# Activation tiles streamed from the last token to the first, from buffers that begin 16 bytes past a multiple of 256

## The reference, cut to what matters

```python
def sq_relu_mlp(h, w_up, w_down):
    return jnp.square(jax.nn.relu(h @ w_up)) @ w_down

def conv_ffn(h, w_up, conv_w, w_down):
    up = causal_dwconv(h @ w_up, conv_w)
    a, u = up[..., :D_FF_2], up[..., D_FF_2:]
    return (jax.nn.silu(a) * u) @ w_down
```

## Time and profile before

| what | value |
|---|---|
| runs | 1120.18 and 1120.35 us, median 1120.26 us |
| span of the profiled execution | 1118.6 us, so 1.7 us less than the median of the runs |
| PE busy | 1111.2 us, 99% of the span, 9640 matmuls |
| weight loads (PEld) busy | 1093.5 us, 98%, 9640 loads |
| DVE busy | 851.5 us, 76% |
| ACT busy | 664.8 us, 59% |
| POOL busy | 252.7 us, 23% |
| DMA | 203.28 MB, mean 182 GB/s |

### The profile page before, as it was taken

One profiled execution on the slowest core, in us unless ns is written; L12 is line 12 of the kernel. 1 busy time (PEld: TensorE's weight loads), 2 busy tenths in 40 slices (PEclk: granted clock), 3 DMA queues, 4 the chain that ended last, 5 costly groups with the idle time before them and its releaser, 6 DMA issues.

```text
span 1118.6 us, 26120 instructions
## 1 busy us (share of the span) xinstructions
PE 1111.2 (99%) x9640; PEld 1093.5 (98%) x9640; DVE 851.5 (76%) x1373; ACT 664.8 (59%) x1113; POOL 252.7 (23%) x248
## 2 busy tenths in 40 slices
PE   9999999999999999999999999999999999999998
PEld 8998999999998999999999999999999999999998
DVE  7776977656687977755587699999668888999854
ACT  6566656545578665644556667666455456666544
POOL 0001400000140600011200363544211034444421
PEclk9999999999999999999999999999999999999999
DMA  9542765655653666565564455664667565665461
GB/s 323 189 151 88 220 196 189 203 197 187 166 161 98 196 199 199 161 223 188 157 188 152 150 173 170 207 201 143 199 203 228 175 213 169 202 204 178 150 211 62
DMA packets 206799, 203.28 MB, mean 182 GB/s; under 512 B 9824, under 2 KB 204768, under 8 KB 206736
## 3 DMA queue, kind: packets, MB, share of 16 engines
q1 hardware_dynamic: 206592, 202.22, 56.9%
q10 hardware_dynamic: 144, 0.20, 0.1%
HBM read 201.35 MB, written 1.05 MB: 181 GB/s over the span
## 4 chain that ended last, share of the span: by engine, by line
PE 98%; DMA 1%; DVE 0%; SPq 0%; issue 0%; ACT 0%
PE gemm L772 29%; PE gemm L774 29%; PE gemm L773 29%; PE gemm L804 2%; PE gemm L806 1%; PE gemm L805 1%; PE gemm L781 1%; PE gemm L783 1%; PE gemm L782 1%; PE score L1017 1%; PE gemm L1029 1%; DMA w_raw<-in_w_first 1%; PE score L1152 0%; PE misc L834 0%; PE gemm L1168 0%; PE score L1240 0%
## 5 line engine op out<-in xcount | busy, mean ns | idle before, releaser
L1756 DVE TENSOR_TENSOR w_lo<-w_raw,w_hi 128x1024 fp32r<-128x1024 f32 (+2 forms) x401 | 478.9, 1200 | 140.2 <-ACT w_hi L1349 138.2
L1349 ACT CAST w_hi<-w_raw 128x1024 fp32r<-128x1024 f32 (+2 forms) x401 | 400.3, 1004 | 142.4 <-PE gemm L774 137.0
L772 PE MATMUL gemm<-act_a,w_hi 128*128 128x256 f32 (+1 forms) x1688 | 467.2, 277 | 1.2 <-DVE act_a L1765 0.8
L774 PE MATMUL gemm<-act_a,w_lo 128*128 128x256 f32 (+1 forms) x1688 | 464.8, 275 | 0.0
L773 PE MATMUL gemm<-act_a,w_hi 128*128 128x256 f32 (+1 forms) x1688 | 464.8, 275 | 0.0
L772 PEld LDWEIGHTS gemm<-act_a,w_hi 128*128 128x128 f32 (+1 forms) x1688 | 316.2, 187 | 5.3 <-issue 2.2
L774 PEld LDWEIGHTS gemm<-act_a,w_lo 128*128 128x128 f32 (+1 forms) x1688 | 316.2, 187 | 0.2
L773 PEld LDWEIGHTS gemm<-act_a,w_hi 128*128 128x128 f32 (+1 forms) x1688 | 316.3, 187 | 0.1
L772 PE MATMUL gemm<-hid,w_hi 128*128 128x256 f32 x864 | 238.2, 276 | 0.0
L774 PE MATMUL gemm<-hid,w_lo 128*128 128x256 f32 x864 | 237.8, 275 | 0.0
L773 PE MATMUL gemm<-hid,w_hi 128*128 128x256 f32 x864 | 237.7, 275 | 0.0
(11 more groups left out here) (303 smaller groups left out, 1443.4 us busy)
## 6 DMA issues: line engine op xcount, KB each, us to landing
w_raw<-in_ffn_w_up SPq DMA_DIRECT2D x76, 1024.0 KB, 5.2
w_raw<-in_ffn_w_down SPq DMA_DIRECT2D x32, 1024.0 KB, 5.2
w_raw<-in_gla_w_in SPq DMA_DIRECT2D x12, 1024.0 KB, 5.3
w_raw<-in_ffn_w_down SPq DMA_DIRECT2D x16, 768.0 KB, 4.6
w_raw<-in_sc_w_in SPq DMA_DIRECT2D x12, 1024.0 KB, 5.2
w_raw<-in_fox_w_in SPq DMA_DIRECT2D x10, 1024.0 KB, 7.4
w_raw<-in_ffn_w_down SPq DMA_DIRECT2D x16, 640.0 KB, 4.3
w_raw<-in_fox_w_out SPq DMA_DIRECT2D x4, 1024.0 KB, 5.1
```

Of the source, the lines that this page charges most:

```text
L772: nc.tensor.matmul(ps, wh[:, k, cols], act[:, k0 + k, 0, :], start=start and k == 0, stop=False)
L774: last = nc.tensor.matmul(ps, wl[:, k, cols], act[:, k0 + k, 0, :], start=False, stop=stop and k == nk - 1)
L1349: nc.scalar.copy(split_half(w_hi, nc_, nj), raw_half(nc_, nj)).then_inc(w_hi_ready, 1)
L1756: nc.vector.tensor_tensor(split_half(w_lo, nc_, nj), raw_half(nc_, nj), split_half(w_hi, nc_, nj).bitcast(F32), ALU.subtract).then_inc(w_l ...
```

## The change

`feature_block` and `tile_products` pass the moving operand and the output with the token axis reversed: the access pattern starts at the last of the 256 tokens and steps by -1, in SBUF for the operand and in PSUM for the result. Each token's result lies where it lay before. The four split buffers begin 16 bytes past a multiple of 256 in place of 240. `token_block`, the other matmuls and all other engines' instructions keep their order and form; the stationary activations of `token_block` lie at the new place too, and buffers behind `act_b` move by 32 bytes.

```diff
-        act_a = split_tiles("act_a", KD, past=240)
-        act_b = split_tiles("act_b", KD, past=240)
+        act_a = split_tiles("act_a", KD, past=16)
+        act_b = split_tiles("act_b", KD, past=16)
...
-        hid = split_tiles("hid", DFF // P, past=240)
+        hid = split_tiles("hid", DFF // P, past=16)
...
-        m_act = split_tiles("m_act", 5, past=240)
+        m_act = split_tiles("m_act", 5, past=16)
...
+            def backwards(tokens):
+
+                return tokens[:, ::-1]
+
             def feature_block(ps, c, j, act, k0=0, col=0, start=True, stop=True, tiles=None, rows=P, ahead_of=None):
 
                 wh, wl = split_half(w_hi, c, j), split_half(w_lo, c, j)
-                nk, cols = kind_of(c)[1], slice(col, col + rows)
+                nk, cols, to = kind_of(c)[1], slice(col, col + rows), backwards(ps)
...
-                    nc.tensor.matmul(ps, wh[:, k, cols], act[:, k0 + k, 0, :], start=start and k == 0, stop=False)
-                    nc.tensor.matmul(ps, wh[:, k, cols], act[:, k0 + k, 1, :], start=False, stop=False)
-                    last = nc.tensor.matmul(ps, wl[:, k, cols], act[:, k0 + k, 0, :], start=False,
-                                            stop=stop and k == nk - 1)
+                    high, low = backwards(act[:, k0 + k, 0, :]), backwards(act[:, k0 + k, 1, :])
+                    nc.tensor.matmul(to, wh[:, k, cols], high, start=start and k == 0, stop=False)
+                    nc.tensor.matmul(to, wh[:, k, cols], low, start=False, stop=False)
+                    last = nc.tensor.matmul(to, wl[:, k, cols], high, start=False, stop=stop and k == nk - 1)
...
             def tile_products(ps, c, j, act, k, rows=P):
 
                 wh, wl = split_half(w_hi, c, j)[:, k, 0:rows], split_half(w_lo, c, j)[:, k, 0:rows]
-                nc.tensor.matmul(ps, wh, act[:, k, 0, :], start=k == 0, stop=False)
-                nc.tensor.matmul(ps, wh, act[:, k, 1, :], start=False, stop=False)
-                return nc.tensor.matmul(ps, wl, act[:, k, 0, :], start=False, stop=k == KD - 1)
+                to, high, low = backwards(ps), backwards(act[:, k, 0, :]), backwards(act[:, k, 1, :])
+                nc.tensor.matmul(to, wh, high, start=k == 0, stop=False)
+                nc.tensor.matmul(to, wh, low, start=False, stop=False)
+                return nc.tensor.matmul(to, wl, high, start=False, stop=k == KD - 1)
```

## The result

The changed kernel takes 1176.97 us (1176.89 and 1177.06) against 1120.26 us: ratio 1.0505, 95% interval 1.0475 to 1.0536. It is slower by 56.7 us, outside the range of the prediction.

A forecast was written before the change was run, and what follows sets the result against it. TensorE's own matmul pace was taken to bound the kernel. Terms 8700 x 0 + 408 x 0 = 0 against the profiled 1118.6 us, with 1.7 us around it, gave 1120.3 us; range 1088 to 1157 us, likeliest case 1119 to 1122 us.

The forecast's parts named there:

- What bounds the kernel: Whole span: TensorE's own pace sets nearly every microsecond, 99% busy, 2.6 us of waits; DMA, ACT and DVE don't set the end.
- The other engines' cover: ACT and DVE work stays off the path: DVE's densest stretch 90.72 us of 100, cover gone at 103 ns a matmul.
- The lower bound, 108.1 ns: Pace of 16 matmuls with 64 moving columns, set by weight loads alone; no direction gains over 5.3 ns, 1074 us.
- What the pace answers to: Matmul pace: normal pace same with weight loads of 48 and 128 columns and at another place; excess answers to neither.
- Rows 7: Earlier trace, weights moving and activations stationary, 256 moving columns, another place within 256 bytes: 47 matmuls, 113.6 ns each.
- The reversed read and write: 8700 matmuls with reversed tokens: mirrored stream has the same groups and crossings, so 0 change per matmul.
- The upper bound, +3.9 ns a matmul: Worse phase at 117.3 ns, seen for about a dozen matmuls with full weight loads; over 9108 matmuls 35.5 us, 1156 us.
- Rival 2: Every block of `feature_block`: reversed stream stays in the worse phase, 3.9 ns on each of 8700 matmuls, 1154 us; chance 0.16.
- The same groups and the same crossings: Moving stream: backwards from 16 mirrors forwards from 240, 64 groups of four adjacent values; ground for taking 0.
- Rival 1: Faster: streams stop disturbing each other or a stream's start gets cheaper; 29.6 us gain, 1091 us; beyond 2%, chance 0.30.
- Rival 4: Reversed patterns turned round before TensorE, only buffer place changes; most likely no change, 1119 to 1122 us; within no-change chance 0.40.
- The stationary use of the buffers: 408 matmuls reading activations as weights from the new place: taken as 0, at most 1.6 us.

## Why the prediction was wrong

- **What bounds the kernel: right.** TensorE's pace sets everything: the chain is 98% PE again, waits are 2.4 us in place of 2.6, DVE stayed covered.
- **The other engines' cover: thinner than predicted.** 90.72 us in 100 is not DVE's densest stretch. Before and after, columns as in the earlier trace rows:
```profile
635.00:735.00 100.00, 100.00 (x880) 99.77 (x879) 95.17 (x149) 64.89 (x106) 49.95 (x43) 1.00 0.57 183
...
665.00:765.00 100.00, 100.00 (x834) 99.95 (x833) 91.03 (x141) 62.31 (x103) 45.69 (x41) 1.00 0.52 170
```
At 110.0 ns the first would last 880 x 110.0 ns = 96.8 us, 1.6 us longer than DVE's work, and the cover would go at about 113.6 x 0.952 = 108.2 ns, not at 103 ns. The pace rose, so no run tests it. The new places and orders cost these engines little: over the whole kernel DVE is busy for 856.7 us where it was 851.5, ACT for 662.5 us where it was 664.8, with the same instructions.
- **The lower bound, 108.1 ns: a mean with one short distance in it.** In the earlier trace rows the first two of the 16 matmuls start 57 ns apart, the others 111 to 112 ns; those of the earlier trace rows, with 128 columns, start 109 to 110 ns apart, and most of the products with a single moving column 111 to 112 ns. So with loads of 128 columns this pace does not follow the number of moving columns, which fits the reading that the load sets it; no run shortens the load alone there.
- **What the pace answers to: the failed reading.** The pace of 113.4 ns in all the prediction's products is 100 us over the 882 matmuls of the earlier trace rows. Its 6.7 ns of excess, and 9.95 ns with 512 columns, were reckoned from a pace of the columns alone that no run shows: the lowest pace of 256 moving columns in a long run is 113.3 ns, and 512 columns take 233.2 ns, 3.2 ns more for each half than 113.4. (The measured 6.7 ns of this section and the experiments are 120.00 less 113.33 ns.) From the earlier trace rows the prediction concluded that the excess does not answer to the weight load or to the place. These rows hold for the good distance only. Rows 7 are another alignment, but a pair that happened to run nearly as well; moved to 16 it went to 116.7 ns. Equal paces of two placements in one tuned kernel say nothing about the placements that it doesn't use. And the place of the weights counts for the stream: 32 bytes in it move one stream from 118.7 to 113.3 ns and another from 113.3 to 120.0 ns.
- **"The reversed read and write", the term of 0: wrong for the read, right for the write.** The argument was that backwards from 16 is the mirror image of forwards from 240. It is, for the moving operand alone; the weights were not mirrored with it, and forwards the place of one counts only against the other. That this is why the mirror image fails is argued, not shown. Shown is that the forward stream had one good distance and the backward stream has none: 113.3 ns against 117.7 ns at best with full loads, and against 117.8 ns with loads of 16 columns at other distances. Measured, the term is 8700 x 6.4 ns = 55 us.
- **The upper bound, +3.9 ns a matmul: too low.** It came from the dozen matmuls at 117.3 ns, as if the worst phase that the trace shows were the worst there is. 120.0 ns is reached without a backward step too (distances 0, 80, 96 and 128 forwards).
- **Rival 2 had the right sign and a part of the mechanism**, 1154 us with a chance of 0.16. "The reversed stream stays in the worse phase" fits in that the dozen at another pace is gone. But the pace is 120.0, not 117.3 ns, and about two thirds of the surplus remain with the shortest loads. It was also tied to the direction alone, while the place forwards costs 38.7 us without it.
- **"The same groups and the same crossings": right for steps inside a group alone.** Steps down inside 16 bytes are free (113.3 ns), steps down inside 32 bytes but across 16 are not (116.7 ns), so the 64 groups of four values did not make the reversed read free. Into PSUM a step of -1 costs nothing (ratio 0.9997), and neither do two of the two-level patterns, groups of 4 reversed inside and blocks of 64 taken backwards, 113.3 ns each.
- **Rival 1** found no support: no run has a pace below 113.2 ns, or above 120.0 ns, in a long run of these products. **Rival 4** was wrong in its second half: forwards from 16, held to be "no change most likely", costs 3.4%.
- **The stationary use of the buffers, taken as 0 and bounded by 1.6 us:** 1.0 us, within the bound.

Shown are: at the distance of 112 the operand's direction, not the result's, costs; forwards the good pace goes with that distance to the weights and with no other of the 11 seen; backwards no distance reaches it; at 112 steps down inside 16-byte groups and three large ones are free, and frequent small ones across the groups are not. Open are: what in the read path makes a step down dear, why the distance of 112 bytes alone is good, what else sets the paces between 116.7 and 120.0 ns, and why a load of 64 columns is worse at 112 than one of 128. No run has the stationary operand mirrored too.

## What to carry to other kernels

Where one engine's pace is the time, look for what the pace depends on outside the operands that the trace happens to have: two equal rows in a tuned kernel are one working point, not evidence that a parameter is free. Where a kernel runs at its good distance, stream the moving operand upwards over its 16-byte groups; the order inside 16 bytes (113.3 ns), a few large jumps back (113.3 ns) and the order of the result in PSUM (ratio 0.9997) were free here, and the full reversal cost 6.7 ns. Where it does not, the direction made no consistent difference (116.7 to 120.0 ns both ways). When a buffer that TensorE reads is moved by as little as 16 or 32 bytes, compare the pace per matmul again (distances 96 and 112 forwards: 120.0 and 113.3 ns), and check the distance between the moving and the stationary operand, not the alignment of one.

## What the runs showed of the hardware

- One matmul with 256 columns of float32-rounded data takes 113.3 to 120.0 ns from start to start with full weight loads in long runs; addresses and the order of reading alone move the mean, and besides both ends 116.7, 117.8, 118.3 and 118.7 ns occur.
- The weight place matters as much as the moving operand's: +32 bytes turned 118.7 into 113.3 ns and 113.3 into 120.0 ns.
- A moving operand read backwards takes 117.7 to 120.0 ns at each of 16 distances to the weights; forwards 10 of 11 distances give 116.7 to 120.0 ns too, and 112 bytes give 113.3 ns.
- A result written backwards into PSUM costs nothing: ratio 0.9997 (0.9988 to 1.0007).
- At the good distance, loads of 16, 32, 48 and 128 columns all allow 113.3 ns, but 64 columns, in the one stage where they were run, give 116.7 ns.
